# Attention over selected keys: the normalising pass moves to GpSimd, the copy of the turned weights to VectorE, and the first queries' causal mask into the bias table

## The chip, the cores and the metric

The kernel runs on one core of one Trainium2 chip. The time is device microseconds of one execution. The core has TensorE (matrix products into PSUM, eight banks of 128 partitions by 512 fp32 columns), VectorE, ScalarE and GpSimd (elementwise work; GpSimd works in SBUF only here), and DMA queues. In the profile they are PE (with PEld, its weight loads), DVE, ACT, POOL and SP. Each engine works through its own list of instructions in order; between engines there are only semaphores, which a finished instruction raises and a later one waits for.

## The reference, cut to what matters

Two transformer blocks over 512 tokens of width 1024. The second block's last attention, `dsa_attention`, is the stage in question: 16 heads share one key of 128 features per token, and each query attends to the 128 keys that an index score selected.

```python
def block(args):
    ...
    causal = key_pos[None, :] <= t[:, None]
    isc = jnp.where(causal[None], isc, NEG_2)
    _, sel = lax.top_k(isc, topk)
    valid = sel <= t[None, :, None]
    ...
    logits = jnp.einsum('bqhd,bqkd->bqhk', qb, kg) * scale
    bias = rel_bias[t5_bucket(t[None, :, None] - sel)]
    logits = logits + jnp.swapaxes(bias, -1, -2).astype(jnp.float32)
    logits = jnp.where(valid[:, :, None, :], logits, NEG_2)
    p = jax.nn.softmax(logits, axis=-1)
    return jnp.einsum('bqhk,bqkd->bqhd', p, vg)
```

The kernel does not gather. It computes the scores against all keys up to the query block and adds -1e30 to those not selected. For the first 128 queries all keys up to the query are selected, so their mask is the causal one alone.

## The kernel before, in words

The kernel streams all weights once (299 blocks of 128 by 1024), and GpSimd splits each block into a high and a low part (L857, L859); TensorE multiplies in three passes (L280 to L282). Between two such products, the selected-key attention runs. It is made of 64 **units**: a unit is one head and one block i of 128 queries (i = 0 to 3), with 128(i+1) keys. The order (L436 and before, `units`) goes by pairs of heads: both heads at i=0, both at i=1, both at i=2, both at i=3, then the next pair. So eight units make a **pair of heads**, and there are eight pairs.

What a unit goes through (semaphores `d_scores` to `d_out`):

1. TensorE: scores into one of three banks (L450, two passes in the trace), then the mask of unselected keys is added by an identity product (L452).
2. ScalarE: the scores, scaled, into `tmp`, which has four slots, one for each unit in turn (L515). It waits until the unit four before it has been turned, since that one's slot is taken over.
3. VectorE: adds the relative bias from the tables in `y` and `bias` and takes the row maximum (L492).
4. ScalarE: exponential with the row sum (L521).
5. VectorE: reciprocal of the sum (L499) and the product with it, in place in `tmp` (L501).
6. TensorE: transposes the weights, 128 columns at a time, into bank 3 or 5 (L462). This is called **turning**.
7. ScalarE: copies the turned weights to `probs_t`, four slots (L531).
8. TensorE: the product with the values, for two units at once (L475), into bank 6 or 7.
9. After a pair of heads is complete, ScalarE writes its high part (L1306), VectorE its low part (L647), the input of the next product (`out3`, which begins with L310).

The order on each engine is written out by hand as steps. In step s TensorE does the scores of unit s, turns unit s-3, and in odd steps multiplies the values of units s-5 and s-4. ScalarE does in step s the scaling of unit s, the exponential of s-1, the copy of s-2. VectorE does in step s the bias of unit s, and the reciprocal and the product of s-1. GpSimd has nothing to do in this stage: its next block of the weight stream waits for TensorE to get on with `out3`.

The bias tables come from a product of a one-hot matrix of buckets (`bucket_onehot`, 32 by 640) with `rel_bias`, early in the kernel; the row of every head is stored in DRAM and read back with overlapping strides.

The same functions with `scaled=False` and no `scale` serve the first block's attention (semaphores `a_...`, 32 units, near 150 to 200 us), which is left as it is.

Of the kernel before, what the change touches and what calls it, by code (L numbers as in the profile page):

```python
# [129 lines left out]
def two_blocks(nc, x_in, p_in, vecs_in, stream_in, ada_in, consts_in, bias_in, onehot_in, rel_in, wi_in,  # L130
# [9 lines left out]
    with ctx:  # L140
# [298 lines left out]

        def pe_attention(pe, sems, units, queries, keys, values, probs, mask, evacuated, read="masked"):  # L440
            n = len(units)
            for step in range(n + 4):
                if step < n:
                    h, i = units[step]
                    cols = P * (i + 1)
                    if step >= 3:

                        pe.wait_ge(sems[read], step - 2)
                    b = bank[step % 3]
                    m = pe.matmul(b[:, 0:cols], queries(h, i), keys(h, cols), start=True, stop=mask is None)  # L450
                    if mask is not None:
                        m = pe.matmul(b[:, 0:cols], ident_b[:], mask(i, cols), start=False, stop=True)  # L452
                    m.then_inc(sems["scores"], 1)
                if 3 <= step < n + 3:
                    u = step - 3
                    h, i = units[u]
                    pe.wait_ge(sems["normed"], u + 1)
                    if u >= 2:

                        pe.wait_ge(sems["copied"], u - 1)  # L460
                    for j in range(i + 1):
                        m = pe.transpose(bank[(3, 5)[u % 2]][:, j * P:(j + 1) * P], tmp[:, u % 4, j * P:(j + 1) * P], ident)  # L462
                    m.then_inc(sems["turned"], 1)
                if step >= 4 and step % 2:

                    u = step - 4
                    h, i = units[u]
# [11 lines left out]
        def dve_attention(v, sems, units, tables, base, low=None, scaled=False):  # L479
            for step in range(len(units) + 5):  # L480
                if low is not None and step >= 5 and units[step - 5][0] % 2 and units[step - 5][1] == TT - 1:
                    low(v, units[step - 5][0] // 2)
                if step < len(units):
# [10 lines left out]
                if 1 <= step <= len(units):  # L494
# [4 lines left out]
                    v.reciprocal(rden[:, base + u:base + u + 1], den[:, base + u:base + u + 1]).then_inc(sems["rden"], 1)  # L499
                    v.wait_ge(sems["rden"], u + 1)  # L500
                    v.tensor_scalar(tmp[:, u % 4, 0:cols], tmp[:, u % 4, 0:cols], rden[:, base + u:base + u + 1], None,  # L501
                                    ALU.mult).then_inc(sems["normed"], 1)

        def act_attention(a, sems, units, probs, base, evacuate, scale=None):
            late = scale is not None
            for step in range(len(units) + 3 + late):
                if late and step < len(units):
# [8 lines left out]
                if late <= step < len(units) + late:  # L516
# [5 lines left out]
                                 scale=-1.0, accum_out=den[:, base + u:base + u + 1]).then_inc(sems["exp"], 1)  # L522
                if 1 + late <= step <= len(units) + late:
                    u = step - 1 - late
                    h, i = units[u]
# [5 lines left out]
                    a.activation(probs(u)[:, 0:cols], bank[(3, 5)[u % 2]][:, 0:cols], ACT.Copy).then_inc(sems["copied"], 1)  # L531
                if step >= 3 + late:
                    u = step - 3 - late
                    h, i = units[u]
# [314 lines left out]
        def _(pool):  # L849
# [57 lines left out]
            pool_lows("mix1")  # L907
            split_stream(START["qi"] + SPLIT, START["gu3"] + SPLIT)
            pool_lows("ffn1")
# [4 lines left out]
        def _(pe):  # L914
            pe.wait_ge(masks_ready, 4)
            pe_norm(pe, "pre_mix")
# [3 lines left out]
            for n in range(2):  # L920
                m = pe.matmul(bank[6 + n][0:D_HEADS, 0:SPAN // 2], big_flat[0:BUCKETS, 20 * S + SPAN:20 * S + SPAN + D_HEADS],
                              big_flat[0:BUCKETS, 20 * S + n * (SPAN // 2):20 * S + (n + 1) * (SPAN // 2)], start=True, stop=True)
            m.then_inc(rel_row, 1)
# [114 lines left out]
            for h in range(2):  # L1038
                for t in range(TT):
# [3 lines left out]
                    if h == 0 or t < 3:  # L1043
# [12 lines left out]
                         lambda i, cols: not_selected[:, i, 0:cols],  # L1056
                         lambda c: low_done("dattn", c), read="scaled")
            pe_tiles(pe, "out3", "dattn", norm="ffn1")
# [62 lines left out]
        def _(a):  # L1121
# [6 lines left out]
            a.preload_act_table(ACT.Sqrt)  # L1128
            a.dma_start(big[0:BUCKETS, 20:22, :].rearrange("p c s -> p (c s)")[:, 0:SPAN], onehot_in).then_inc(onehot_landed, 16)
            a.dma_start(big[0:BUCKETS, 20:22, :].rearrange("p c s -> p (c s)")[:, SPAN:SPAN + D_HEADS], rel_in).then_inc(onehot_landed, 16)  # L1130
# [245 lines left out]
        def _(v):  # L1376
            v.wait_ge(consts_landed, 16)
            v.tensor_copy(ident_b[:], ident).then_inc(masks_ready, 1)
            v.tensor_copy(strict_b[:], strict).then_inc(masks_ready, 1)
# [225 lines left out]
def bucket_onehot():  # L1605
# [6 lines left out]
    hot = (np.arange(BUCKETS)[:, None] == bucket[None, :]) & (np.arange(SPAN) >= P - 1)[None, :]  # L1612
    return hot.astype(np.float32)

# [93 lines left out]
```

## Time and profile before

| what | us |
|---|---|
| median of 3 runs | 2167.24 (2165.22 to 2168.67) |
| the profiled execution's own time | 2167.39 |
| its span | 2165.6 |
| selected-key attention, first scores to the first product of `out3` | 1642.13 to 1747.49 |
| PE busy over the span | 2034.1 (94%) |
| ACT busy over the span | 603.3 (28%) |
| DVE busy over the span | 1034.0 (48%) |
| POOL busy over the span | 1215.7 (56%) |

The span is the time from the first to the last instruction of one profiled execution. Times of the trace are microseconds from the span's start. A busy share over the span is a mean over stages that differ much; the attention has to be read from its own rows. The granted clock (PEclk) is 1.00 where TensorE had its full 2.4 GHz.

### The profile page before, as it was taken

The numbers are of one execution on the slowest core, as the hardware profiler recorded it, in microseconds if no ns is written. First come the engines' busy times: TensorE is split into PE (matmuls) and PEld (weight loads), VectorE is DVE, ScalarE is ACT, GpSimd is POOL, SyncE is SP. The second block draws the span as 40 slices with busy tenths as digits, with TensorE's granted clock in tenths as the row PEclk, the third lists the DMA queues.
The fourth block names the chain that finished last, engine by engine and source line by source line (L and its number), as shares of the span: only waits on it lengthen the run. The fifth ranks groups of instructions, "written<-read, shape, count | busy, mean of one in ns | idle before, by whom it ended". The sixth has DMA issues, their size and how long they took to land.

```text
span 2165.6 us, 26887 instructions
## 1 busy us (share of the span) xinstructions
PE 2034.1 (94%) x9346; PEld 1624.7 (75%) x9346; DVE 1034.0 (48%) x1611; ACT 603.3 (28%) x1134; POOL 1215.7 (56%) x678
## 2 busy tenths in 40 slices
PE   5999799997998899899899999999999998999999
PEld 4876678886887677666788888878686577888887
DVE  4456469989225800365443333131784744333422
ACT  2226210000113320597231111121316823111210
POOL 6650568886663766433566666654352046666664
PEclk9999889999998899999999999988999999999999
DMA  6330258887231222100423333321121012333331
GB/s 232 127 117 1 78 172 287 287 286 248 87 97 49 78 97 92 45 1 0 156 78 97 97 97 93 95 84 49 60 77 40 1 55 73 97 97 97 97 97 68
DMA packets 62327, 221.15 MB, mean 102 GB/s; under 512 B 6913, under 2 KB 7169, under 8 KB 62129
## 3 DMA queue, kind: packets, MB, share of 16 engines
q1 hardware_dynamic: 44928, 161.25, 23.4%
q10 hardware_dynamic: 17328, 58.95, 7.7%
q8 instruction: 46, 0.75, 0.1%
q14 instruction: 25, 0.20, 0.0%
HBM read 218.03 MB, written 2.14 MB: 102 GB/s over the span
## 4 chain that ended last, share of the span: by engine, by line
PE 62%; ACT 6%; DVE 6%; issue 2%; DMA 0%; POOL 0%; ACTq 0%; DVEq 0%
PE bank L280 17%; PE bank L281 17%; PE bank L282 17%; PE bank L310 1%; PE bank L315 1%; PE bank L311 1%; PE bank L588 1%; ACT y L658 1%; ACT L666 1%; PE bank L381 1%; PE bank L450 1%; PE bank L475 1%; DVE big L1530 1%; ACT tmp L515 1%; ACT tmp L521 1%
## 5 line engine op out<-in xcount | busy, mean ns | idle before, releaser
L280 PE MATMUL bank<-a_hi,w_hi 128*128 128x512 f32 x2072 | 813.3, 393 | 10.3 <-DVE a_lo L812 4.9
L282 PE MATMUL bank<-a_hi,w_lo 128*128 128x512 f32 x2072 | 808.5, 390 | 0.0
L281 PE MATMUL bank<-a_lo,w_hi 128*128 128x512 f32 x2072 | 808.5, 390 | 0.0
L857 POOL TENSOR_SCALAR w_hi<-raw 128x1024 fp32r<-128x1024 f32 x299 | 356.9, 1194 | 755.7 <-PE bank L282 496.0
L859 POOL TENSOR_TENSOR w_lo<-raw,w_hi 128x1024 fp32r<-128x1024 f32 x299 | 764.9, 2558 | 24.9
L280 PEld LDWEIGHTS bank<-a_hi,w_hi 128*128 128x128 f32 x2072 | 390.4, 188 | 94.1 <-POOL w_lo L859 5.5
L282 PEld LDWEIGHTS bank<-a_hi,w_lo 128*128 128x128 f32 x2072 | 390.3, 188 | 81.9
L281 PEld LDWEIGHTS bank<-a_lo,w_hi 128*128 128x128 f32 x2072 | 390.5, 188 | 81.2 <-issue 0.7
L1334 DVE CUSTOM_DVE_ANT_0 y<-y,cond 128x1024 f32<-128x1024 f32 x96 | 212.7, 2267 | 0.5 <-DMA y<-in_ada 0.5
L1345 DVE SCALAR_TENSOR_TENSOR tmp<-bank,vecs,tmp 128x511 f32<-128x511 f32 x88 | 66.0, 750 | 263.1 <-ACT tmp L1093 263.1
L1093 ACT ACTIVATE tmp<-bank,vecs 128x512 f32<-128x512 f32 x88 | 68.5, 781 | 372.2 <-PE bank L282 364.6
L812 DVE TENSOR_TENSOR a_lo<-big,a_hi 128x512 fp32r<-128x512 f32 x63 | 64.8, 1040 | 223.8 <-ACT a_hi L807 223.8
L807 ACT ACTIVATE a_hi<-big 128x512 fp32r<-128x512 f32 x63 | 38.9, 631 | 262.0 <-PE bank L282 262.0
L903 POOL TENSOR_TENSOR a_lo<-y,a_hi 128x512 fp32r<-128x512 f32 (+1 forms) x48 | 52.5, 1093 | 80.4 <-DVE a_hi L642 80.4
L631 DVE TENSOR_SCALAR y<-bank 128x512 uint32<-128x512 uint32 (+1 forms) x48 | 27.2, 593 | 134.5 <-PE bank L590 133.8
L737 DVE TENSOR_TENSOR square_sum<-square_sum,squares 128x512 f32<-128x512 f32 x45 | 65.3, 1450 | 48.5 <-ACT squares L692 47.3
L310 PE MATMUL bank<-a_hi,w_hi 128*128 128x512 f32 x160 | 70.0, 437 | 11.1 <-ACT a_hi L774 6.8
L1196 ACT ACTIVATE tmp<-bank 128x512 f32<-128x512 f32 x22 | 13.2, 599 | 229.0 <-DVE ada_part L1334 223.3
L1348 DVE SCALAR_TENSOR_TENSOR tmp<-bank,vecs,tmp 128x510 f32<-128x510 f32 x88 | 65.9, 749 | 12.0 <-DVE tmp L1345 3.0
L381 PE MATMUL bank<-consts,square_sum 128*128 128x1 f32 x216 | 36.4, 295 | 35.6 <-DVE square_sum L737 31.9
L752 POOL TENSOR_TENSOR a_lo<-tmp,a_hi 128x512 fp32r<-128x512 f32 x24 | 32.0, 1333 | 66.6 <-ACT tmp L778 36.8
L311 PE MATMUL bank<-a_hi,w_lo 128*128 128x512 f32 x160 | 68.0, 425 | 0.0
(207 smaller groups left out, 2307.2 us busy)
## 6 DMA issues: line engine op xcount, KB each, us to landing
raw<-in_stream SPq DMA_DIRECT2D x299, 512.0 KB, 3.5
y<-in_ada ACTq DMA_DIRECT2D x96, 512.0 KB, 4.7
x<-in_x SPq DMA_DIRECT2D x4, 512.0 KB, 7.1
bias<-in_bias ACTq DMA_DIRECT2D x1, 2048.0 KB, 14.1
y<-rel_rows ACTq DMA_DIRECT2D x1, 2048.0 KB, 9.4
bias<-rel_rows ACTq DMA_DIRECT2D x1, 2048.0 KB, 14.2
out<-x SPq DMA_DIRECT2D x8, 256.0 KB, 2.1
cond<-in_c ACTq DMA_DIRECT2D x1, 512.0 KB, 9.2
```

Source lines behind the costliest of these rows:

```text
L280: pe.matmul(o, lhs_hi, rhs_hi, start=start, stop=False, **kw)
L281: pe.matmul(o, lhs_hi, rhs_lo, start=False, stop=False, **kw)
L282: return pe.matmul(o, lhs_lo, rhs_hi, start=False, stop=stop, **kw)
L310: pe.matmul(o[:], w_hi[:, s, cols], a_hi[:, k, :], start=start and k == chunks[0], stop=False, skip_group_check=True)
L311: pe.matmul(o[:], w_lo[:, s, cols], a_hi[:, k, :], start=False, stop=False, skip_group_check=True)
L737: v.tensor_tensor(group, group, squares[:, added % 2, :], ALU.add).then_inc(sq_added, 1)
L857: pool.tensor_scalar(w_hi[:, s, :], raw[:, j, :], 1.0, 1.0, ALU.mult, ALU.mult).then_inc(high_ready, 1)
L859: pool.tensor_tensor(w_lo[:, s, :], raw[:, j, :], f32(w_hi[:, s, :]), ALU.subtract).then_inc(split_ready, 1)
L1093: a.activation(tmp[:, n, :], bank[n][:], ACT.Identity, bias=vecs[:, bass.ds(r * 16 + (col + 3), 1)], scale=vecs[:, bass.ds(r * 16 + (col + ...
L1334: v.tensor_tensor_reduce(w, w, cond[:], 1.0, 0.0, ALU.mult, ALU.add, ada_part[:, part:part + 1]).then_inc(ada_done, 1)
L1345: v.scalar_tensor_tensor(tmp[:, n, 1:S], bank[n][:, 0:S - 1], vecs[:, bass.ds(r * 16 + (col + 1), 1)], tmp[:, n, 1:S], ALU.mult, ALU.add). ...
L1348: v.scalar_tensor_tensor(tmp[:, n, 2:S], bank[n][:, 0:S - 2], vecs[:, bass.ds(r * 16 + col, 1)], tmp[:, n, 2:S], ALU.mult, ALU.add).then_i ...
```

## The change

In the selected-key attention only: the product with the reciprocal goes from VectorE to GpSimd (`pool_normalise`), the copy of the turned weights from ScalarE to VectorE. TensorE turns unit s-4 in step s instead of s-3 (`lag=4`), and multiplies the values of units s-6 and s-5 in even steps. VectorE does in step s the bias of unit s, the reciprocal of s-1 and then the copy of s-4; ScalarE does the scaling of unit s and the exponential of s-1, and the high part of a finished pair two steps later than before; VectorE its low part three steps later. GpSimd's weight stream is cut in two loops, and its 64 products stand between them.

The mask product L452 is left out for i=0. Instead the one-hot matrix has a 33rd row that is 1 where the key lies ahead of the query, and a row of -1e30 stands under `rel_bias`, so that the table holds the causal mask. This costs one memset of one partition by 16 columns on VectorE at the kernel's start.

```diff
-            for step in range(n + 4):
+            for step in range(n + lag + 1):
...
-                    m = pe.matmul(b[:, 0:cols], queries(h, i), keys(h, cols), start=True, stop=mask is None)
-                    if mask is not None:
+
+                    masked = mask is not None and i
+                    m = pe.matmul(b[:, 0:cols], queries(h, i), keys(h, cols), start=True, stop=not masked)
+                    if masked:
                         m = pe.matmul(b[:, 0:cols], ident_b[:], mask(i, cols), start=False, stop=True)
                     m.then_inc(sems["scores"], 1)
-                if 3 <= step < n + 3:
-                    u = step - 3
+                if lag <= step < n + lag:
+                    u = step - lag
...
-                if step >= 4 and step % 2:
-
-                    u = step - 4
+                u = step - lag - 1
+                if u >= 0 and u % 2:
+
...
         def dve_attention(v, sems, units, tables, base, low=None, scaled=False):
...
-                    v.wait_ge(sems["rden"], u + 1)
-                    v.tensor_scalar(tmp[:, u % 4, 0:cols], tmp[:, u % 4, 0:cols], rden[:, base + u:base + u + 1], None,
-                                    ALU.mult).then_inc(sems["normed"], 1)
+                    if not scaled:
+                        v.wait_ge(sems["rden"], u + 1)
+                        v.tensor_scalar(tmp[:, u % 4, 0:cols], tmp[:, u % 4, 0:cols], rden[:, base + u:base + u + 1], None,
+                                        ALU.mult).then_inc(sems["normed"], 1)
+                if scaled and 4 <= step < len(units) + 4:
+                    u = step - 4
+                    h, i = units[u]
+                    cols = P * (i + 1)
+                    v.wait_ge(sems["turned"], u + 1)
+                    if u >= 4:
+
+                        v.wait_ge(sems["out"], u - 3)
+                    v.tensor_copy(probs_t[:, u % 4, 0:cols], bank[(3, 5)[u % 2]][:, 0:cols]).then_inc(sems["copied"], 1)
+
+        def pool_normalise(pool, sems, units, base):
+            for u, (h, i) in enumerate(units):
+                cols = P * (i + 1)
+                pool.wait_ge(sems["rden"], u + 1)
+                pool.tensor_scalar(tmp[:, u % 4, 0:cols], tmp[:, u % 4, 0:cols], rden[:, base + u:base + u + 1], 1.0,
+                                   ALU.mult, ALU.mult).then_inc(sems["normed"], 1)
...
         def act_attention(a, sems, units, probs, base, evacuate, scale=None):
             late = scale is not None
-            for step in range(len(units) + 3 + late):
+            behind = 6 if late else 3
+            for step in range(len(units) + behind):
...
-                if 1 + late <= step <= len(units) + late:
-                    u = step - 1 - late
+                if not late and 1 <= step <= len(units):
+                    u = step - 1
...
-            split_stream(START["qi"] + SPLIT, START["gu3"] + SPLIT)
+            split_stream(START["qi"] + SPLIT, START["out3"] + SPLIT)
+
+            pool_normalise(pool, d_sems, d_units, n_stat // 2)
+            split_stream(START["out3"] + SPLIT, START["gu3"] + SPLIT)
```

VectorE's list in the steps in which both units of a pair stand at i=2 (384 columns), before; brackets hold the semaphores waited for:

```order
L492 ISA tmp,neg_max<-tmp,y 128x384 [waits d_scaled]
L492 ISA neg_max 128x1
L499 RECIPROCAL rden<-den 128x1 [waits d_exp]
L501 TENSOR_SCALAR tmp<-tmp,rden 128x256 [waits d_rden]
L492 ISA tmp,neg_max<-tmp,y 128x384 [waits d_scaled]
L492 ISA neg_max 128x1
L499 RECIPROCAL rden<-den 128x1 [waits d_exp]
L501 TENSOR_SCALAR tmp<-tmp,rden 128x384 [waits d_rden]
```

and the same place after:

```order
L494 ISA tmp,neg_max<-tmp,y 128x384 [waits d_scaled]
L494 ISA neg_max 128x1
L501 RECIPROCAL rden<-den 128x1 [waits d_exp]
L514 COPY probs_t<-bank3 128x128 [waits d_out,d_turned]
L494 ISA tmp,neg_max<-tmp,y 128x384 [waits d_scaled]
L494 ISA neg_max 128x1
L501 RECIPROCAL rden<-den 128x1 [waits d_exp]
L514 COPY probs_t<-bank5 128x128 [waits d_out,d_turned]
```

The copy, of a unit four steps back, stands where the product stood, behind the bias of the newest unit and the reciprocal of the one before it.

TensorE's list where the scores of a new pair of heads begin (i=0, then i=1), before:

```order
L450 MATMUL bank1<-k_lat,big 128x128 [waits d_scaled]
L452 MATMUL bank1<-not_selected,ident_b 128x128
L462 MATMUL bank5<-consts,tmp 128x128 [waits d_copied,d_normed]
L462 MATMUL bank5<-consts,tmp 128x128 x2
L450 MATMUL bank2<-k_lat,big 128x128 [waits d_scaled]
L452 MATMUL bank2<-not_selected,ident_b 128x128
L462 MATMUL bank3<-consts,tmp 128x128 [waits d_copied,d_normed]
L462 MATMUL bank3<-consts,tmp 128x128 x3
L475 MATMUL bank7<-probs_t,big 64x128 [waits d_copied]
L475 MATMUL bank7<-probs_t,big 64x128 x5
```

and after:

```order
L452 MATMUL bank1<-k_lat,big 128x128 [waits d_scaled]
L464 MATMUL bank3<-consts,tmp 128x128 [waits d_copied,d_normed]
L464 MATMUL bank3<-consts,tmp 128x128 x2
L477 MATMUL bank7<-probs_t,big 64x128 [waits d_copied]
L477 MATMUL bank7<-probs_t,big 64x128 x3
L452 MATMUL bank2<-k_lat,big 128x128 [waits d_scaled]
L464 MATMUL bank5<-consts,tmp 128x128 [waits d_copied,d_normed]
L464 MATMUL bank5<-consts,tmp 128x128 x2
L452 MATMUL bank0<-k_lat,big 128x256 [waits d_scaled]
L454 MATMUL bank0<-not_selected,ident_b 128x256
L464 MATMUL bank3<-consts,tmp 128x128 [waits d_copied,d_normed]
```

The mask product at i=0 is gone, turning comes a step later, and the product with the values has moved from the odd steps to the even ones.

## Rows read from the trace of the kernel before

**Rows 1.** Waits within 1641.5 to 1749, engine and line waited for: us, times, longest

```profile
DVE tmp L492 <- ACT tmp L515: 22.5, 33, 5.0
PEld bank L462 <- DVE tmp L501: 20.3, 26, 2.6
```

**Rows 2.** Stretches: us, busy PE, PEld, DVE, ACT, POOL (count), PEclk, DMA share, GB/s

```profile
1655.00:1667.50 12.50, 11.59 (x86) 7.30 (x85) 8.71 (x34) 11.10 (x34) 0.00 (x0) 1.00 0.00 1
900.00:904.00 4.00, 2.22 (x14) 1.60 (x14) 3.26 (x6) 3.97 (x7) 1.90 (x2) 0.99 0.00 0
1649.00:1652.00 3.00, 3.00 (x13) 1.48 (x12) 1.69 (x8) 1.45 (x4) 0.00 (x0) 0.67 0.00 0
```

**Rows 3.** Timeline, marks: start us, us, engine line operation out<-in count [idle before <-releaser]

```profile
1653.95 0.70 ACT L515 ACTIVATE tmp<-bank,squares 128x512 f32<-128x512 f32 x1
...
1741.57 0.69 ACT L515 ACTIVATE tmp<-bank,squares 128x512 f32<-128x512 f32 x1
...
1747.49 0.50 PE L310 MATMUL bank<-a_hi,w_hi 128*128 128x512 f32 x1
```

**Rows 4.** Timeline of one pair of heads, rows chosen

```profile
1675.12 0.44 PE L475 MATMUL bank<-probs_t,big 128*64 128x128 f32 x4
...
1675.49 1.12 PE L450 MATMUL bank<-k_lat,big 128*128 128x512 f32 x2
...
1678.98 0.70 ACT L515 ACTIVATE tmp<-bank,squares 128x512 f32<-128x512 f32 x1
...
1679.05 0.49 PE L450 MATMUL bank<-k_lat,big 128*128 128x128 f32 x2
...
1679.45 0.55 PE L462 MATMUL bank<-consts,tmp 128*128 128x128 f32 x3
1679.55 0.73 ACT L521 ACTIVATE tmp<-tmp,neg_max 128x512 f32<-128x512 f32 x1
1679.71 0.69 DVE L492 CUSTOM_DVE_ANT_0 tmp<-tmp,y 128x512 f32<-128x512 f32 x1 [0.32 <-ACT tmp L515]
...
1680.41 0.16 DVE L499 RECIPROCAL rden<-den 128x1 f32<-128x1 f32 x1
1680.61 0.49 DVE L501 TENSOR_SCALAR tmp<-tmp,rden 128x512 f32<-128x512 f32 x1
...
1682.34 0.36 ACT L515 ACTIVATE tmp<-bank,squares 128x128 f32<-128x128 f32 x1
1682.54 0.30 PEld L450 LDWEIGHTS bank<-k_lat,big 128*128 128x128 f32 x2 [0.17 <-issue]
...
1682.59 0.40 ACT L521 ACTIVATE tmp<-tmp,neg_max 128x128 f32<-128x128 f32 x1
...
1683.11 0.16 DVE L499 RECIPROCAL rden<-den 128x1 f32<-128x1 f32 x1
1683.19 0.60 PE L462 MATMUL bank<-consts,tmp 128*128 128x128 f32 x4
...
1683.83 0.60 ACT L531 ACTIVATE probs_t<-bank 128x512 f32<-128x512 f32 x1 [0.74 <-PE bank L462]
...
1684.47 0.85 PEld L475 LDWEIGHTS bank<-probs_t,big 128*64 128x64 f32 x16 [0.27 <-ACT probs_t L531]
...
1685.50 0.91 PE L450 MATMUL bank<-k_lat,big 128*128 128x384 f32 x2
...
1686.41 0.27 PE L462 MATMUL bank<-consts,tmp 128*128 128x128 f32 x1
```

**Rows 5.** Groups by line and shape, VectorE reading PSUM: busy us, mean ns

```profile
L631 DVE TENSOR_SCALAR y<-bank 128x512 uint32<-128x512 uint32 x32 | 21.9, 685 | 134.2 <-PE bank L590 133.4
...
L631 DVE TENSOR_SCALAR y<-bank 128x256 uint32<-128x256 uint32 x16 | 6.6, 409 | 0.3 <-PE bank L590 0.3
```

**Rows 6.** Timeline, GpSimd and VectorE at the same time

```profile
1446.52 1.05 POOL L857 TENSOR_SCALAR w_hi<-raw 128x1024 fp32r<-128x1024 f32 x1 [3.34 <-issue]
...
1447.13 0.97 DVE L737 TENSOR_TENSOR square_sum<-square_sum,squares 128x512 f32<-128x512 f32 x1
```

More of the change, by code:

```diff
@@ L438, in out_bank, with pe_attention @@
             return bank[6 + (h // 2) % 2]
-        def pe_attention(pe, sems, units, queries, keys, values, probs, mask, evacuated, read="masked"):
+        def pe_attention(pe, sems, units, queries, keys, values, probs, mask, evacuated, read="masked", lag=3):
             n = len(units)
-            for step in range(n + 4):
+            for step in range(n + lag + 1):
                 if step < n:
@@ L479, in dve_attention @@
         def dve_attention(v, sems, units, tables, base, low=None, scaled=False):
-            for step in range(len(units) + 5):
-                if low is not None and step >= 5 and units[step - 5][0] % 2 and units[step - 5][1] == TT - 1:
-                    low(v, units[step - 5][0] // 2)
+            for step in range(len(units) + (8 if low is not None else 1)):
+                if low is not None and step >= 8 and units[step - 8][0] % 2 and units[step - 8][1] == TT - 1:
+                    low(v, units[step - 8][0] // 2)
                 if step < len(units):
@@ L531, in act_attention @@
                     a.activation(probs(u)[:, 0:cols], bank[(3, 5)[u % 2]][:, 0:cols], ACT.Copy).then_inc(sems["copied"], 1)
-                if step >= 3 + late:
-                    u = step - 3 - late
+                if step >= behind:
+                    u = step - behind
                     h, i = units[u]
@@ L914, in _ @@
         def _(pe):
-            pe.wait_ge(masks_ready, 4)
+            pe.wait_ge(masks_ready, 5)
             pe_norm(pe, "pre_mix")
@@ L1056, in _ @@
                          lambda i, cols: not_selected[:, i, 0:cols],
-                         lambda c: low_done("dattn", c), read="scaled")
+                         lambda c: low_done("dattn", c), read="scaled", lag=4)
             pe_tiles(pe, "out3", "dattn", norm="ffn1")
@@ L1377, in _ @@
             v.wait_ge(consts_landed, 16)
+            v.memset(big[BUCKETS:BUCKETS + 1, 21, SPAN - S:SPAN - S + D_HEADS], NEG).then_inc(masks_ready, 1)
             v.tensor_copy(ident_b[:], ident).then_inc(masks_ready, 1)
@@ L1612, in bucket_onehot @@
     hot = (np.arange(BUCKETS)[:, None] == bucket[None, :]) & (np.arange(SPAN) >= P - 1)[None, :]
-    return hot.astype(np.float32)
+    ahead = (np.arange(SPAN) < P - 1)[None, :]
+    return np.concatenate([hot, ahead]).astype(np.float32)
 def tile_blocks(w):
```

6 lines of the change are left out of this document (3 added, 3 removed).

## The prediction, made before the changed kernel was timed

> **What bounds the kernel now.** Only one stage changes, the selected-key attention, so I read the stage and not the page's shares. The first stretch, 12.5 us of steady work [rows 2], shows ScalarE busy for 11.10 and TensorE for 11.59 at full clock, GpSimd for nothing. The waits [rows 1] say what ends idle time: VectorE waits 22.5 us for ScalarE's scaling, TensorE's loads 20.3 us for VectorE's product with the reciprocal. So the two engines hold each other: ScalarE has three passes per unit and is nearly full, its exponential is late, and TensorE stands before turning. From the scaling of unit 7 to that of unit 63, which are seven pairs of heads, 1741.57 - 1653.95 = 87.62 us pass [rows 3], 12.52 us a pair. From the scaling of unit 63 to `out3` another 5.92 us.
>
> If nothing on another engine were waited for, TensorE would need less. Its pieces [rows 4], each from its first row to that of the next piece: scores and mask up to turning 0.40 (128 columns; about 0.30 without the mask), 0.65 (256; 1682.54 to 1683.19), 0.91 (384; 1685.50 to 1686.41), and by the same step 1.17 for 512; another 0.11 per 128 columns turned, (0.60 - 0.27)/3; values 0.37 for i=0 (1675.12 to 1675.49) and 1.03 for i=3 (1684.47 to 1685.50), between them 0.59 and 0.80. A pair: 2 x 3.03 + 20 x 0.11 + 2.79 = 11.05 us. That is the most that the change can reach, 1.47 us a pair.
>
> **What is removed and moved.** ScalarE loses 64 copies, and that removes the present bound. VectorE loses 64 products and gains 64 copies from PSUM; the only rows of such a read are 0.685 us for 512 columns and 0.409 for 256 [rows 5], hence 0.54 for 384 and 0.28 for 128. That is nearly what the products took (0.49 for 512 [rows 4]), so VectorE's busy time hardly changes. GpSimd was idle [rows 2], its product of 512 columns costs at least half of 1.05 us, the 1024-column row [rows 6], and at most all of it; I take 0.6. Turning comes a step later, and in the loops below a GpSimd product started after its reciprocal has more than 2 us before TensorE wants it, so even 1.05 is hidden. The 16 mask products save 0.10 each where TensorE is on the path, which is one in each pair: 0.8 us in all, contained in the 0.30 above. The memset at the start is bounded by a small VectorE operation, 0.16 us, and stands before work that waits for the input: nothing. The extra row of the one-hot input is 2.5 KB in a transfer of 80: nothing. GpSimd's 64 products stand where its stream waits for TensorE anyway.
>
> **What is added: a wait in series.** This is the step that decides. Follow the order of VectorE: bias of unit s, reciprocal of s-1, copy of s-4. TensorE multiplies values in even steps s, and needs the copy of s-5, which VectorE does in its step s-1, behind the bias of unit s-1. That bias needs the scaling of s-1, and the scaling needs the slot in `tmp` that unit s-5 has left, so it waits until s-5 is turned. Before, ScalarE copied a unit as soon as it was turned. Now between turning and the copy of the same unit stand: scaling of s-1; then in parallel the bias of s-1 and the exponential of s-2; then the reciprocal of s-2; then the copy. TensorE meanwhile does only scores of s and turning of s-4, then stands. After the values, it does scores of s+1 and turns s-3, and the loop closes. Everything in it is in series, so its length is the time of two steps.
>
> Terms, all from [rows 4]: turned to scaling 0.04 (1683.19 + 0.60 to 1683.83). Scaling to exponential 0.25 (128; 1682.34 to 1682.59) and 0.57 (512; 1678.98 to 1679.55), between them 0.36 and 0.47. Exponential to reciprocal 0.52 (128; 1682.59 to 1683.11) and 0.86 (512; 1679.55 to 1680.41), between them 0.63 and 0.75. The other branch, scaling to bias to reciprocal, is 0.73 + 0.70 = 1.43 for 512 (1678.98, 1679.71, 1680.41), the same as 0.57 + 0.86, so it adds nothing. Reciprocal to copy: 0.20 where the second waited for the first (1680.41 to 1680.61); the copy doesn't, I take 0.15. Copy to values 0.04 (1683.83 + 0.60 to 1684.47).
>
> The four loops of a pair, in the order: turned, scaling and exponential, reciprocal, copy, gap, values, scores, turning:
> - s=2: 0.04 + 0.77 + 0.15 + 0.54 + 0.04 + 0.80 + 0.65 + 0.60 = 3.59
> - s=4: 0.04 + 0.99 + 0.15 + 0.68 + 0.04 + 1.03 + 0.91 + 0.27 = 4.11
> - s=6: 0.04 + 1.22 + 0.15 + 0.28 + 0.04 + 0.37 + 1.17 + 0.38 = 3.65
> - s=8: 0.04 + 1.43 + 0.15 + 0.41 + 0.04 + 0.59 + 0.30 + 0.49 = 3.45
>
> Sum 14.80 us a pair against 12.52. In the third and fourth loop ScalarE's and VectorE's high and low parts of a finished pair fall into times in which the next term isn't yet due.
>
> Seven pairs: 7 x (14.80 - 12.52) = +16.0. The fill, before values are multiplied, gets shorter, since ScalarE has no copies between its first passes: six of them at 0.3 to 0.6, of which I count -1.2 (0 to -2). The drain after unit 63 is scaled has the last two multiplications of values behind two copies each and one GpSimd product: 6.8 instead of 5.92, +0.9 (0 to +1.6). Sum **+15.7**. On the profiled execution, 2167.39, which stands 0.15 above the median of the runs, that gives 2183.1, on the median 2182.9: **2183 us**. Each loop is good to 0.15, a pair to 0.6, seven pairs to 4.2, with the ends 6: 2177 to 2189.
>
> **Rivals.**
>
> *A, faster: the series isn't binding.* If the copy is done by the time TensorE asks for it, TensorE is the bound at 11.05 a pair: 7 x (-1.47) - 1.2 + 0.9 = -10.6, or 2157. For it: ScalarE loses a third of its passes, TensorE has that much idle time. Against: the copy would have to be finished within 0.6 to 1.4 us of turning (scores and turning of one step), and the sum of the terms before it is 1.5 to 2.3. Chance 0.08.
>
> *B, no difference: the series binds, but its terms overlap more than rows of a full ScalarE show.* ScalarE will stand idle in front of its scaling, and its starts may come sooner. It takes 0.57 less in every loop to come out at 12.5 a pair: 2167. For 0.57 almost a third of the terms outside TensorE would have to go. Chance 0.07.
>
> *C, slower still: GpSimd and VectorE hold each other.* In [rows 6] VectorE's product of two tensors in SBUF starts at 1447.13 beside a GpSimd product of one tensor that runs until 1447.57, and ends at 1448.10: it got going when GpSimd was through. L492 also reads two tensors of SBUF, and GpSimd's new product starts beside it. By my loops that product begins about 0.25 after a reciprocal and the bias that follows it begins after the copy, 0.43 to 0.83 after; at 0.6 us the overlap is small and falls on the even units, which have slack. If the product takes 1.05 it reaches into the bias of odd units too, about one hold of 1 us a pair: +8, 2191. It decides if the GpSimd product of 512 columns takes more than about 0.9. Chance 0.06.
>
> The Trainium skill speaks here against the change: "GPSIMD Engine Reference", section 8, says that GpSimd shares its SBUF interfaces with VectorE and contends with instructions that have two SBUF inputs or run in a two-port mode. By that rule each of the 64 bias passes can be hit; by the row's hold and the order of events few are, and the sum stays. The trace agrees with the rule, with the 0.97 us row.
>
> *D, the clock.* TensorE idles more, 25% of each pair. At 1649 to 1652 the granted clock was 0.67 of full [rows 2] after the standstill at the stage's start. But in 900 to 904 it was 0.99 with TensorE busy for 2.22 of 4.00 us, so pauses of a microsecond don't lower it there. If a third of the stage ran at the lower of the two levels (1.2 instead of 2.4 GHz), TensorE's terms in the loops, 7.56 a pair, would double there: 8 x 7.56 / 3 = +20, 2203. Chance 0.03.
>
> **The numbers.** Forecast mechanism 0.76, A 0.08, B 0.07, C 0.06, D 0.03. The range reaches from 2170 to 2192: it leaves out A, B and D, and the thin ends of the forecast's own range. A measurement of this kernel can tell 0.2%, or 4.3 us. Slower by more than that: forecast, C and D, 0.85. Faster: A, 0.08. Within: B, 0.07.
>
> **What would show each step.** VectorE's copy should stand late: TensorE's largest wait in the stage should be the values (L477) for the copy (L514), about 0.5 to 1.7 us at each even step, some 30 us in all, and turning should hardly wait for GpSimd. ScalarE should be busy for about 8.5 of 14.8 us, and its scaling (L535) should wait for turning (L464). The time of seven pairs between the scalings of unit 7 and unit 63 should be about 104 us. L520 should take 0.5 to 0.7 us at 512 columns, and the L494 rows 0.69 with few held ones. I am wrong if L477 doesn't wait for L514, if L520 takes over 0.9, or if the stage's clock isn't 1.00.

## The result, and the profile after

| what | before | after |
|---|---|---|
| median of 4 runs each, us | 2167.95 (2165.22 to 2168.92) | 2186.16 (2180.77 to 2192.8) |
| profiled execution's own time | 2167.39 | 2180.77 |
| its span | 2165.6 | 2179.0 |
| stage: first scores to first product of `out3` | 105.36 | 121.01 |
| of it: fill, seven pairs, drain | 11.82, 87.62, 5.92 | 9.84, 104.14, 7.03 |

The changed kernel is slower: ratio 1.0087, 95% interval 1.0058 to 1.0117. A second measurement of it (below) gives 1.0083, 1.0062 to 1.0104.

The lines of the stage have moved: scores L452, mask L454, turning L464, values L477, bias L494, reciprocal L501, VectorE's copy L514, GpSimd's product L520, scaling L535, exponential L541. The marks of the stage, as in [rows 3], from the timeline of after (start us, duration us, engine, line, operation, tiles, count, idle time before and what ended it): first scores, scaling of unit 7, scaling of unit 63, first product of `out3`.

```profile
1639.90 0.71 PE L452 MATMUL bank<-k_lat,big 128*128 128x128 f32 x4 [0.69 <-ACT big L1326]
1649.74 0.69 ACT L535 ACTIVATE tmp<-bank,squares 128x512 f32<-128x512 f32 x1 [1.21 <-PE bank L464]
1753.88 0.69 ACT L535 ACTIVATE tmp<-bank,squares 128x512 f32<-128x512 f32 x1 [0.83 <-PE bank L464]
1760.91 0.50 PE L310 MATMUL bank<-a_hi,w_hi 128*128 128x512 f32 x1
```

So 1753.88 - 1749.74 = 104.14 us for seven pairs, 14.88 a pair. The waits of the whole stage, 1641.5 to 1765 (engine and line waited for: us in total, times, longest), answer to [rows 1]:

```profile
POOL tmp L520 <- DVE rden L501: 80.0, 64, 2.7
DVE tmp L494 <- ACT tmp L535: 46.7, 40, 4.9
ACT tmp L535 <- PE bank L464: 44.0, 36, 2.1
PEld bank L477 <- DVE probs_t L514: 35.8, 32, 1.8
PE bank L477 <- DVE probs_t L514: 27.7, 31, 1.6
```

Every engine now waits for the next one in a ring. TensorE stands in front of the values for VectorE's copy, 32 times, once per step in which it multiplies values. ScalarE stands in front of its scaling for the turning that frees the slot. VectorE stands in front of its bias for the scaling. The largest line, GpSimd's 80.0 us, is idle time of an engine that almost nobody waits for: TensorE's products wait for L520 1.8 us in one place, its loads 2.9 us in three.

Two stretches of after, as in [rows 2] (us, busy PE, PEld, DVE, ACT, POOL with counts, granted clock, DMA share, GB/s), the first of them about one pair:

```profile
1683.60:1698.00 14.40, 10.85 (x80) 6.87 (x79) 8.75 (x33) 8.29 (x25) 4.25 (x8) 1.00 0.01 2
1649.00:1652.00 3.00, 1.49 (x15) 1.14 (x15) 1.63 (x6) 2.26 (x6) 1.03 (x2) 1.00 0.00 0
```

No engine is full: TensorE 75%, VectorE 61%, ScalarE 58%. The chain of what ended last, in order of time (start us, us, what; the pieces of a few hundredths between engines left out), shows one loop:

```profile
1682.96 0.37 ACT tmp L535
1683.33 0.39 ACT tmp L541 x2
...
1683.74 0.04 DVE rden L501
...
1683.83 0.57 DVE probs_t L514
...
1684.44 0.88 PE bank L477 x12
1685.31 0.63 PE bank L452 x2
1685.94 0.11 PE bank L454
1686.05 0.45 PE bank L464 x4
...
1686.59 0.47 ACT tmp L535
```

Read from top to bottom it is: scaling, exponential, reciprocal, copy, values, scores, mask, turning, and again scaling. It goes through three engines in series. While the other two work, TensorE has only the scores and the turning of one more unit to do and stands idle for the rest: 1.00 us before the values at 1688.40.

### The profile page after: what moved, and what is told of

The parts are those of the page before. It is cut to its first block, busy times and chain, and to the rows that moved or that the text cites. A ratio compares the mean times of both kernels' runs of the same rounds, so it can differ in the third digit from the quotient of the medians.

```text
span 2179.0 us, 26857 instructions
## 1 busy us (share of the span) xinstructions
PE 2028.2 (93%) x9330; PEld 1622.4 (74%) x9330; DVE 1037.0 (48%) x1612; ACT 583.9 (27%) x1070; POOL 1248.6 (57%) x742
## 4 chain that ended last, share of the span: by engine, by line
PE 62%; DVE 6%; ACT 5%; issue 2%; DMA 0%; POOL 0%; ACTq 0%; DVEq 0%
PE bank L280 17%; PE bank L282 17%; PE bank L281 17%; PE bank L310 1%; PE bank L315 1%; PE bank L311 1%; PE bank L608 1%; PE bank L477 1%; PE bank L452 1%; ACT y L678 1%; ACT L686 1%; ACT tmp L535 1%; DVE probs_t L514 1%; PE bank L381 1%; DVE big L1555 1%
## 5 line engine op out<-in xcount | busy, mean ns | idle before, releaser
L520 POOL TENSOR_SCALAR tmp<-tmp,rden 128x128 f32<-128x128 f32 (+3 forms) x64 | 34.2, 535 | 80.0 <-DVE rden L501 80.0
```

## The experiments

A pair of heads in the seven-pair stretch is the measure, since in the profiles of the same code it repeats far better than the whole time does: 104.14, 104.14 us for the changed kernel, 87.62, 87.58 for the one before. All orders side by side, from the profiled executions:

| kernel | us a pair | seven pairs | fill | drain |
|---|---|---|---|---|
| before | 12.52 | 87.62 | 11.82 | 5.92 |
| e10, before again | 12.51 | 87.58 | 11.82 | 5.93 |
| e4, mask in the table alone | 12.52 | 87.61 | 10.54 | 5.92 |
| e5, e4 + product on GpSimd | 12.96 | 90.70 | 11.96 | 6.19 |
| changed kernel | 14.88 | 104.14 | 9.84 | 7.03 |
| e0, changed again | 14.88 | 104.14 | 9.84 | 7.04 |
| e9, changed, mask products kept | 14.94 | 104.60 | 9.85 | 7.03 |
| e3, changed, 2 columns on GpSimd | 14.88 | 104.15 | 9.74 | 7.03 |
| e8, changed, copy ahead of reciprocal | 14.05 | 98.38 | 9.57 | 6.87 |
| e2, changed, six slots | 13.55 | 94.83 | 9.56 | 7.04 |
| e7, copy in front, product on VectorE | 12.58 | 88.06 | 9.27 | 7.33 |
| e1, copy in front | 11.53 | 80.72 | 9.03 | 6.28 |
| e6, copy in front and six slots | 11.34 | 79.40 | 8.75 | 6.37 |

### e0: the changed kernel again

> The changed kernel once more, to see what of its time is the attention stage and what is not. In its first profile seven pairs of heads took 104.1 us (scaling of unit 7 to scaling of unit 63) where the kernel before took 87.6, which is the 14.88 against 12.52 us a pair that the four loops gave. Theory (the copy stands in series behind bias, exponential and reciprocal): 104.1 again within 0.5, whatever the whole time is; whole time 2180 to 2193. If the seven pairs themselves vary by several us from one execution to the next, the series isn't what sets them.

Measured: median 2184.29 (6 runs), before 2168.05 (15 runs), ratio 1.0083 (1.0062 to 1.0104); stage 121.02. The first scores stand at 1641.04 instead of 1639.90, seven pairs are the same to the hundredth.

### e1: VectorE's copy of s-4 in front of the bias of s

The changed kernel with one block of lines moved; nothing else.

```diff
+                if scaled and 4 <= step < len(units) + 4:
+                    u = step - 4
...
+                    v.tensor_copy(probs_t[:, u % 4, 0:cols], bank[(3, 5)[u % 2]][:, 0:cols]).then_inc(sems["copied"], 1)
                 if step < len(units):
                     u = step
...
-                if scaled and 4 <= step < len(units) + 4:
-                    u = step - 4
...
-                    v.tensor_copy(probs_t[:, u % 4, 0:cols], bank[(3, 5)[u % 2]][:, 0:cols]).then_inc(sems["copied"], 1)
```

> The changed kernel, with VectorE's copy of unit s-4 moved to the front of its step s, ahead of the bias of unit s. Everything else, GpSimd's product too, is as changed. Theory (series): between turning and the values now stands the copy alone (0.04 + 0.28 to 0.69 + 0.04), most of it beside scores and turning of TensorE, so TensorE becomes the bound: 11.1 to 11.6 us a pair, seven pairs 78 to 81, whole time 2154 to 2160. Rival (GpSimd and VectorE hold each other over SBUF): the holds stay as they are, so a pair stays within 0.5 us of 14.88. Rival (no engine is the cause but latency of GpSimd's product before turning): the same, no gain.

Measured: median 2159.79 (2152.91 to 2161.39, 10 runs), ratio 0.9962 (0.9947 to 0.9977); seven pairs 1733.91 - 1653.19 = 80.72. The two scalings that mark them, and then the busy time and the waits within 1655 to 1735 (the copy is L493 here, the bias L503, the reciprocal L510):

```profile
1653.19 0.69 ACT L535 ACTIVATE tmp<-bank,squares 128x512 f32<-128x512 f32 x1 [0.58 <-PE bank L464]
1733.91 0.69 ACT L535 ACTIVATE tmp<-bank,squares 128x512 f32<-128x512 f32 x1 [0.32 <-PE bank L464]
```

```profile
1655.00:1735.00 80.00, 76.42 (x557) 50.06 (x564) 61.84 (x229) 60.67 (x173) 29.82 (x56) 1.00 0.01 1
```

```profile
ACT tmp L535 <- PE bank L464: 19.1, 27, 1.2
PEld bank L477 <- DVE probs_t L493: 7.6, 21, 0.9
```

The same instructions on the same engines, 3.35 us a pair less: what made the changed kernel slow is the copy's place in VectorE's list, not the engine that does it. TensorE's loads wait for it 7.6 us in these 80 us; in the changed kernel it was 24.0 us in the same 80. TensorE is busy for 76.42 of 80 us, so this order is close to TensorE's own limit, and it beats both kernels.

### e2: six slots for the weights

The order of the changed kernel, but `tmp` gets two more slots from a tile that is free in this stage, and the scaling of s waits for the turning of s-6 instead of s-4.

```diff
+        def slot(sems, u):
+            if sems is not d_sems:
+                return tmp[:, u % 4, :]
+            return tmp[:, u % 6, :] if u % 6 < 4 else square_sum[:, u % 6 - 4, :]
...
-                    if u >= 4:
+                    if u >= 6:
...
-                        a.wait_ge(sems["turned"], u - 3)
+                        a.wait_ge(sems["turned"], u - 5)
```

> The changed kernel with its order untouched, but six slots for the scaled scores instead of four (two more in a buffer that is idle in this stage), so that the scaling of unit s waits for the turning of s-6 instead of s-4. This takes the other link out of the same loop. Theory (series): turning of s-5 no longer has scaling and bias of s-1 behind it, they have run before, so the copy follows turning at once: 11.1 to 12.2 us a pair, seven pairs 78 to 85. Rival (the copy's place alone costs the time, whatever the slots): near 14.88 a pair. Rival (holds between GpSimd and VectorE): at least 14 a pair.

Measured: seven pairs 94.83, a miss: I expected the ring to be cut, and it only got shorter by 1.33 us a pair. The waits within 1655 to 1735 and the chain say why (values L482, copy L519, scaling L540, mask L459, scores L457, exponential L546):

```profile
PEld bank L482 <- DVE probs_t L519: 19.3, 24, 1.5
ACT tmp L540 <- PE bank L459: 15.5, 16, 1.6
```

```profile
1683.30 0.88 PE bank L482 x12
1684.18 0.63 PE bank L457 x2
1684.81 0.12 PE bank L459
...
1684.96 0.03 ACT tmp L540
...
1685.33 0.60 ACT tmp L546 x2
...
1686.03 0.70 DVE probs_t L519
...
1686.77 1.09 PE bank L482 x16
```

The scaling no longer waits for a turning, but for the scores of its own unit, which TensorE does after the values. Those scores stand right in front of the turning in TensorE's list, so the ring closes one item earlier and loses the turning alone: from the first values to the next values 3.47 us here (1683.30 to 1686.77) against 3.96 in the changed kernel (1684.44 to 1688.40). The four loops of a pair lose 0.28, 0.39, 0.50 and 0.17 us, in the order of their turnings of two, three, four and one times 128 columns. A ring in lists that are worked in order has more than one link between two engines; with one taken out, the next one holds.

### e3: GpSimd's product of two columns

The changed kernel, where GpSimd normalises only the first two columns of each unit (that part of the computation is left out), so that its product is short and can't hold VectorE.

```diff
         def pool_normalise(pool, sems, units, base):
...
-                cols = P * (i + 1)
+                cols = 2
```

> The changed kernel, where GpSimd's product covers two columns of each unit and leaves the others unnormalised, so it takes about 0.1 to 0.2 us instead of 0.39 to 0.69 and holds VectorE hardly at all. This leaves out part of the computation, to see what GpSimd's part costs in time. Theory (series): GpSimd isn't in the loop; a pair stays at 14.88 within 0.2, seven pairs 103 to 104.5. Rival (holds): VectorE's held bias passes (0.67 instead of 0.29 at 128 columns) are set free; if they are what costs the time, seven pairs drop by 5 us or more, towards 87.

Measured: seven pairs 104.15 against 104.14. GpSimd's product in this kernel (durations min/median/max in ns); I had expected 0.1 to 0.2 us:

```profile
L520 POOL TENSOR_SCALAR tmp<-tmp,rden x64: 267/268/272, 1640.6 to 1753.0; 128x2 f32<-128x2 f32 x64
```

In the changed kernel the first of the two biases of 128 columns in a pair runs beside a product of 512 columns and takes 0.67 us (the pair of rows stands under "The hold", below). At the same place here:

```profile
1677.77 0.27 POOL L520 TENSOR_SCALAR tmp<-tmp,rden 128x2 f32<-128x2 f32 x1 [1.93 <-DVE rden L501]
1677.93 0.28 DVE L494 CUSTOM_DVE_ANT_0 tmp<-tmp,y 128x128 f32<-128x128 f32 x1
```

VectorE is held by GpSimd in the changed kernel, 0.67 us for what takes 0.28 without, seven times in the stage at this place; and neither that nor the product's own length costs the stage anything: both fall into slack.

### e4 and e5: two parts of the change on the kernel before

e4 takes the mask part alone. e5 adds GpSimd's product; the copies stay on ScalarE and turning stays at s-3.

```diff
-                    if mask is not None:
+                    masked = mask is not None and i
+                    if masked:
...
-    return hot.astype(np.float32)
+    ahead = (np.arange(SPAN) < P - 1)[None, :]
+    return np.concatenate([hot, ahead]).astype(np.float32)
```

and in e5 besides:

```diff
-                    v.wait_ge(sems["rden"], u + 1)
-                    v.tensor_scalar(tmp[:, u % 4, 0:cols], tmp[:, u % 4, 0:cols], rden[:, base + u:base + u + 1], None,
-                                    ALU.mult).then_inc(sems["normed"], 1)
+                    if not scaled:
+                        v.wait_ge(sems["rden"], u + 1)
...
+            pool_normalise(pool, d_sems, d_units, n_stat // 2)
```

> The kernel before with the mask part of the change alone (the table holds the first queries' causal mask, 16 identity products of 128 columns go). Theory: each spares TensorE 0.10 us, at most two of them in a pair where TensorE is on the chain, none where ScalarE is: seven pairs 86.2 to 87.6 against 87.62 (gain 0 to 1.4). Rival (the mask's product counts more, for it adds a wait or a weight load): below 86. It can't be slower than 87.7 by either.

Measured: seven pairs 87.61. The sixteen mask products are worth nothing in the steady part of the kernel before.

> The kernel before with two parts of the change alone: the mask in the table and the product on GpSimd; the copies stay on ScalarE, turning stays at s-3. Theory: ScalarE bounded the kernel before together with the chain scaling, bias, exponential, reciprocal, product, turning; GpSimd's product is 0.2 us longer at each width (0.69 against 0.49 at 512 columns) and stands in that chain, so this part alone gains nothing: 12.5 to 13.2 us a pair (before: 12.52), seven pairs 87.5 to 92.5. Rival (what slows the changed kernel is GpSimd's product, not the copy's place): 14 us a pair or more, seven pairs 98 or more.

Measured: seven pairs 90.70. The waits within 1655 to 1735 (turning L463, product L510) and the busy time:

```profile
PEld bank L463 <- POOL tmp L510: 17.9, 31, 1.2
```

```profile
1655.00:1735.00 80.00, 71.06 (x499) 44.52 (x501) 36.01 (x157) 69.48 (x205) 26.53 (x50) 1.00 0.00 1
```

ScalarE stays at 87% busy, and TensorE's loads wait 17.9 us for GpSimd's product, where in the kernel before they waited 14.0 us for VectorE's in the same 80 us. Here the product lies in the chain, and GpSimd's is the longer one (0.69 against 0.49 us for 512 columns [rows 4]): +0.44 us a pair. VectorE, which has been relieved, was not the bound.

### e7: the copy in front, the product back on VectorE

Against e1:

```diff
-                    if not scaled:
-                        v.wait_ge(sems["rden"], u + 1)
...
+                    v.wait_ge(sems["rden"], u + 1)
...
-            pool_normalise(pool, d_sems, d_units, n_stat // 2)
```

> The order with the copy in front, but the product with the reciprocal back on VectorE, so that GpSimd does nothing in the stage. This asks what the move to GpSimd is worth once the copy stands right. VectorE's work in a pair: 8.75 us of 14.4 in the changed kernel's window, or about 9.0 a pair, plus 8 products (0.18, 0.28, 0.38, 0.49 for 128 to 512 columns, twice each: 2.7), so 11.7 to 12.0 and the product now stands in VectorE's line ahead of the turning. Theory: VectorE becomes the bound, or nearly, 12.2 to 13.4 us a pair, seven pairs 85 to 94, against 80.72 with GpSimd's product. Rival (GpSimd's help is of no use, TensorE bounds both): 11.3 to 11.7 a pair, seven pairs 79 to 82.

Measured: seven pairs 88.06, 12.58 a pair. Busy time and waits within 1655 to 1735:

```profile
1655.00:1735.00 80.00, 71.09 (x519) 46.47 (x523) 71.31 (x261) 56.87 (x157) 0.00 (x0) 1.00 0.00 1
```

```profile
PEld bank L477 <- DVE probs_t L493: 13.0, 19, 1.1
```

VectorE is at 89% and TensorE at 89%. So with the copy well placed, GpSimd's help is worth 12.58 - 11.53 = 1.05 us a pair. Without it, the move of the copies alone (12.58) only exchanges one nearly full engine for another (before: 12.52). Turning a step later with the copies left on ScalarE was not tried by itself.

### e8: the copy ahead of the reciprocal

Against the changed kernel, the copy's block goes up by one place and stays behind the bias:

```diff
                 if step < len(units):
...
+                if scaled and 4 <= step < len(units) + 4:
...
                 if 1 <= step <= len(units):
...
-                if scaled and 4 <= step < len(units) + 4:
```

> VectorE's list in step s becomes bias of s, copy of s-4, reciprocal of s-1: the copy still stands behind the newest unit's bias, but no longer behind the reciprocal and so no longer behind the exponential of s-2. Theory (the whole chain turned, scaling, bias, exponential, reciprocal, copy is in series): in the changed kernel both branches (exponential then reciprocal, and bias then reciprocal) end together, so what goes is the reciprocal, 0.15 to 0.16 us, and the gap behind it, 0.08, in each of four loops: 14.88 becomes 13.9 to 14.1 us a pair, seven pairs 97 to 99. If the exponential were the true last link: a gain of 0.3 or more per loop, seven pairs below 95. If the place of the bias were of no matter and only the reciprocal's wait bound: seven pairs near those of the copy in front, 80 to 84.

Measured: seven pairs 98.38. That is 0.21 us for each of 28 loops, the reciprocal (0.16) and the little that stood around it. By loop it is 0.25, 0.22, 0.19 and 0.17 us for scalings of 128, 256, 384 and 512 columns. So the exponential, which the copy no longer follows, ended with the bias or less than 0.1 us behind it (in the changed kernel at 1683.71 against 1683.66 for 128 columns), nearly as the sum had it; what remains is the wait behind the bias, and it is the larger part: from here to e1 another 2.5 us a pair go.

### e9: the mask products kept

```diff
-                    masked = mask is not None and i
+                    masked = mask is not None
...
-    ahead = (np.arange(SPAN) < P - 1)[None, :]
+    ahead = np.zeros(SPAN)[None, :]
```

> The changed kernel with the identity products of the first query block put back and the 33rd row of the one-hot matrix all zero. In the changed kernel's series TensorE's scores stand in the loop only for one of the two units of a size; the other's are done while TensorE waits for the copy. Theory: one mask product a pair counts, 0.10 us: seven pairs 104.14 + 0.7 = 104.8 (104.6 to 105.0). Rival 1 (both count, the scores of both units lie in the series): 105.4 to 105.7. Rival 2 (TensorE's work is hidden altogether): 104.1 to 104.2.

Measured: 104.60, at the lower edge of what was expected: 0.07 us a pair, less than the 0.10 of one mask product, and far from the 0.2 of two. In a ring of which TensorE's scores are part, the mask is worth something; in the kernel before (e4) it was worth nothing.

### e6: the copy in front, and six slots

e1 and e2 together: both diffs stand above.

> Copy in front and six slots for the weights, so that the scaling waits for the turning of two units earlier. In the kernel with the copy in front ScalarE's scaling still waits 19.1 us for turning in 80 us, and a pair takes 11.53 us against 11.05 us of TensorE's own pieces. Theory (TensorE is nearly the bound there, and what is left is in part this wait): 11.1 to 11.45 us a pair, seven pairs 77.7 to 80.2, ratio of the whole time 0.994 to 0.9965. Rival (the wait of the scaling lies in ScalarE's slack): no change against 80.72, ratio 0.9962.

Measured: seven pairs 79.40, median 2160.71 (2155.54 to 2162.02, 6 runs), ratio 0.9961 (0.9948 to 0.9974). Busy time within 1655 to 1735:

```profile
1655.00:1735.00 80.00, 78.16 (x570) 51.46 (x576) 62.56 (x232) 61.99 (x178) 30.24 (x57) 1.00 0.01 1
```

TensorE is busy for 98% and a pair takes 11.34 us. The 1.3 us that seven pairs gain over e1 can't be seen in the whole time; e1 and e6 are equal there.

### e10: the kernel before once more, for its fill

> The kernel before once more, for its fill. Its profile showed the fill (first scores to the scaling of unit 7) at 11.82 us with a granted clock of 1.00, 0.74 and 0.69 in the windows after the first scores; the kernel with the mask part alone showed 10.54 at 1.00 throughout. Theory (the fall of the clock belongs to single executions, not to the kernel, and costs about 1.3 us): if the clock is 1.00 in the fill this time, the fill is 10.4 to 10.7; if it falls again, 11.7 to 11.9. Rival (the mask products lengthen the fill): about 11.8 with the clock at 1.00. In either case seven pairs 87.6, drain 5.92.

Measured: fill 11.82 again. Two windows of its fill:

```profile
1646.00:1649.00 3.00, 2.27 (x8) 1.18 (x9) 2.21 (x11) 2.81 (x12) 0.00 (x0) 0.84 0.56 175
1649.00:1652.00 3.00, 3.00 (x10) 1.40 (x10) 2.04 (x8) 1.79 (x6) 0.00 (x0) 0.59 0.00 0
```

So the fall of the clock in the fill is not an accident of one execution, as I had supposed: it came in both profiles of this kernel, and e5 shows it too (0.74 and 0.69 in 1647.2 to 1653.2, fill 11.96). e5 has no mask products at i=0 either, so they are not what makes the fill long. e4 differs from the kernel before by 16 mask products only, had the clock at 1.00 and a fill of 10.54. What the clock costs can be read from the same scores, the second of 384 columns, in the kernel before and in e4:

```profile
1647.46 1.36 PE L450 MATMUL bank<-k_lat,big 128*128 128x384 f32 x2
```

```profile
1648.73 0.81 PE L451 MATMUL bank<-k_lat,big 128*128 128x384 f32 x2
```

None of the nine profiles of orders with the copy on VectorE had it. Whether e4 escapes always or once, one execution doesn't tell.

## Why the prediction was right

The forecast was 2183 us and slower; the runs gave 2186.16 and 2184.29. By its own steps:

**The series.** The step that decided holds as written. The turnings end at 1682.87, 1686.49, 1690.61, 1694.27 and 1697.75, so the four loops take 3.62, 4.12, 3.66 and 3.48 us; the terms gave 3.59, 4.11, 3.65 and 3.45. A sum of eight terms came within 0.03 us of each. Most of them are good because each was read for its own column count: scaling to reciprocal, values and turning are right to 0.01, the scores to 0.03. That the sums are as good is luck in part, since two terms err by more and offset each other: turned to scaling takes 0.09 to 0.10 instead of 0.04, reciprocal to copy 0.08 to 0.09 instead of 0.15. The copy with the gap behind it takes 0.02 to 0.03 more than the terms had. Seven pairs: +16.5, forecast +16.0. e1 shows the cause: the same operations without the series take 80.72. e8 takes one link out and gets that link's time back.

**The copy's cost.** [Rows 5] gave 0.68 and 0.41 us for 512 and 256 columns, the interpolation 0.54 and 0.28. L514 takes 690, 413, 546 and 279 ns on average for 512, 256, 384 and 128 columns.

**GpSimd's product.** Taken at 0.6 for 512 columns, between 0.5 and 1.05. It takes 0.69 (585, 477 and 371 ns for 384, 256 and 128). The term was a little low and counts nothing, as said: e3 makes the product 268 ns and nothing moves.

**The hold (rival C).** It exists. At one place in each pair the bias of 128 columns starts 0.16 us after GpSimd's product of 512 columns and ends 0.14 us after it:

```profile
1681.16 0.69 POOL L520 TENSOR_SCALAR tmp<-tmp,rden 128x512 f32<-128x512 f32 x1 [1.61 <-DVE rden L501]
1681.32 0.67 DVE L494 CUSTOM_DVE_ANT_0 tmp<-tmp,y 128x128 f32<-128x128 f32 x1
```

In e1 both biases of 128 columns of a pair are held; they start 0.28 to 0.30 us after the product and take 0.54 to 0.55 us, and again they end 0.14 us after it. So the end of a held bias is set by the end of GpSimd's product and not by its own start. In e8 the bias comes first, and then it is GpSimd that is held: its product of 256 columns takes 0.73 us here, 0.48 where it runs alone, while the bias of 384 columns keeps its 0.56 us:

```profile
1662.70 0.56 DVE L494 CUSTOM_DVE_ANT_0 tmp<-tmp,y 128x384 f32<-128x384 f32 x1
1662.88 0.73 POOL L520 TENSOR_SCALAR tmp<-tmp,rden 128x256 f32<-128x256 f32 x1 [1.96 <-DVE rden L510]
```

"Few held" was right, and that they fall on even units with slack too. C's mechanism was present and its price nil; its point of decision, 0.9 us, was not reached. The rule of the Trainium skill that speaks against the change ("GPSIMD Engine Reference", section 8: GpSimd's SBUF interfaces are VectorE's too, and it contends with instructions of two SBUF inputs) agrees with the trace, 0.67 against 0.28 us, but decides nothing in this order.

**The mask.** 0.10 for one product a pair; e9 gives 0.07 a pair. In the kernel before the same term is nought (e4).

**The fill and the drain.** Fill -1.98, forecast -1.2 (0 to -2): the term was low by 0.8. At the same clock of 1.00 it is 9.84 against e4's 10.54, which is -0.7 for the order. The other 1.3 came with the clock, which stood at 0.67 in the stretch of [rows 2] and at 0.76 in the one ahead of it, and which stayed at 1.00 in the fill after. The stretch ahead, in the kernel before:

```profile
1646.00:1649.00 3.00, 2.63 (x9) 1.36 (x10) 2.40 (x10) 2.80 (x11) 0.00 (x0) 0.76 0.52 175
```

I had read the row only for what the clock might do to the new kernel, not for what its absence would give. Drain 7.03 against 6.8, +1.1 instead of +0.9. Sum for the stage: 16.52 - 1.98 + 1.11 = +15.65, forecast +15.7. That the sum hits to 0.05 is luck: the errors are +0.5, -0.8 and +0.2. Of the fill's -1.98 the order alone gave -0.7, less than the -1.2 forecast; the rest is the clock, which the forecast didn't count.

**The whole time.** The medians lie 16.2 and 18.2 us above those of before, the profiled spans 13.4. The stage hardly varies between profiles of one kernel; what does is the time ahead of it, with the first scores anywhere between 1636.6 and 1647.2 us in the profiles of these kernels, while from `out3` to the end it is 418.0 to 419.4. What varies ahead of the stage was not looked into.

**The other rivals.** A (TensorE the bound at 11.05 a pair) was a real possibility of this work, in another order: e1 and e6 come to 11.53 and 11.34, and whole times of 2159.8 and 2160.7 against its 2157. The reason given against A holds, though the terms before the copy's end add up to 2.03 at most by the loops of the prediction and not to 2.3. B fell: only the reciprocal-to-copy term shrank, by 0.07 of the 0.57 that it needed. D fell: 1.00 in all windows. But its row of reassurance, 900 to 904 at 0.99, was read without its neighbours. Just ahead of it, in the kernel before:

```profile
892.00:896.00 4.00, 0.26 (x2) 0.00 (x0) 3.18 (x5) 2.81 (x5) 1.80 (x2) 1.00 0.00 0
896.00:900.00 4.00, 3.76 (x15) 3.56 (x16) 1.98 (x4) 2.86 (x5) 1.47 (x2) 0.58 0.00 0
```

There the clock did fall, after TensorE had been busy for 0.26 of 4.00 us.

**What would show each step.** L477 was to wait for L514 some 30 us in all; PE has 27.7, its loads 35.8. The 7 pairs were to take about 104. ScalarE was to be busy for 8.5 of 14.8 us; it is 8.29 of 14.40, which is 8.6.

## What to carry to other kernels

When work moves to another engine, its place in that engine's list counts before its duration: the copy cost VectorE little more than it had cost ScalarE (0.69 against 0.60 us for 512 columns), and standing behind or in front of one operation of a newer unit was worth 3.35 us of 14.88. Follow each moved operation backwards through everything that its new engine does ahead of it, until the chain comes back to the engine that waits; if it does, and if that ring is longer than what the fullest engine has to do in it, the length of the ring is the time, whatever the busy shares say (14.88 us a pair with no engine above 75%). Taking one link out with more buffers only helps up to the next link between the same engines, so look for the second one before paying for the slots.

## What the runs showed of the hardware

- GpSimd's product of one tensor by a scalar takes 268, 371, 477, 585 and 692 ns for 2, 128, 256, 384 and 512 columns: 0.84 ns a column, (692 - 371)/384, and 0.26 us whatever the size. VectorE's product took 0.49 us for 512 columns [rows 4]. I had expected half the 1024-column row or all of it; it was about two thirds.
- A bias on VectorE that runs into GpSimd's product is held until the product is through, and ends 0.14, 0.27, 0.40 and 0.54 us after it for 128, 256, 384 and 512 columns, wherever it started. The figures for 128 and 384 repeat in every steady pair of e1; those for 256 and 512 were seen only at the start of the stage. That is about what its columns alone take, 1.07 ns each, (691 - 281)/384; the 0.14 us that a bias takes besides had passed by then. [Rows 6] fit this: 1448.10 - 1447.57 = 0.53 us for 512 columns. Where the product ended within 0.05 us of the bias's start (384 columns in the changed kernel), nothing was lost. In e8, where the bias came first, GpSimd was held instead.
- In e1 both biases of 128 columns in a pair are held (0.54 to 0.55 us instead of 0.28), in the changed kernel one (0.67), and e1's order is still the faster.
- TensorE, idle for a quarter of each pair (10.85 of 14.40 us busy), kept a granted clock of 1.00 throughout the stage. In the kernel before the clock fell in the fill in both profiles, after a stretch with 2.02 of 4.00 us busy (1642 to 1646) and a pause of 2.23 us that ended at 1646.37; in e4 a pause of 2.43 us at the same place was followed by no fall, nor was 1.49 of 3.00 us busy in the changed kernel. What tells these apart the runs don't show.
